# A two-layer hybrid decoder trunk on one core: the mixer's border and first levels in another order, 64 standing columns at the level of 64, and four long products ahead of the four short ones where weights stand

## The reference

```
x = x + 0.5 * rmsnorm(swiglu(rmsnorm(x, g1), w_gate, w_up, w_down), p1)          # 1024 -> 2816 -> 1024
z = rmsnorm(x, g2) @ w_in            # retention q,k,v,gate | GLA q,k,v, low-rank gate, gate
ro = retention(rope(rq), rope(rk) * 64**-0.5, rv)       # 4 heads, keys 64, values 128, fixed decay
log_a = log_sigmoid(ga @ w_a2 + b_a2) / 16
go = gla(gq * 64**-0.5, gk, gv, log_a)                  # 4 heads, decay that depends on the data
x = x + rmsnorm(concat([rmsnorm(ro) * silu(rg), rmsnorm(go) * silu(gg)]) @ w_out, p2)
x = x + rmsnorm(cross_attention(rmsnorm(x, g3), rmsnorm(mem, gm), w_q, w_kv, w_o), p3)   # 4 heads
x = x + 0.5 * rmsnorm(swiglu(rmsnorm(x, g4), ...), p4)
```

## Time and profile before

| | us |
|---|---|
| median of 3 runs | 1184.18 (1184.04 to 1184.34) |
| the profiled execution | 1184.15 |
| its span in the trace | 1182.1 |
| TensorE busy | 1172.7 (99%) |
| VectorE busy | 841.4 (71%) |
| ScalarE busy | 702.6 (59%) |
| GpSimd busy | 150.4 (13%) |
| long products, weights standing in feed-forward, L760 | 864 |
| short ones, L761 | 864 |
| the same in column passes, L639 and L643 | 256 and 256 |

### The profile page before, as it was taken

One profiled execution on the slowest core, in us unless ns is written; L12 is line 12 of the kernel. 1 busy time (PEld: TensorE's weight loads), 2 busy tenths in 40 slices (PEclk: granted clock), 3 DMA queues, 4 the chain that ended last, 5 costly groups with the idle time before them and its releaser, 6 DMA issues. The chain is left out here.

```text
span 1182.1 us, 17336 instructions
## 1 busy us (share of the span) xinstructions
PE 1172.7 (99%) x6164; PEld 997.3 (84%) x6164; DVE 841.4 (71%) x1300; ACT 702.6 (59%) x1225; POOL 150.4 (13%) x220
## 2 busy tenths in 40 slices
PE   9999999999999999999999999999999999999998
PEld 7888888788888888888888888887888888888886
DVE  6866656888767678775487875479887676777752
ACT  7655545756666557654476764376567565666641
POOL 3000002573100100000000000036431001000000
PEclk9999999999999999999999999999999999999999
DMA  9756554454545365555465555554545454555540
GB/s 358 271 184 235 194 202 160 175 179 143 195 144 178 131 204 199 178 201 209 142 214 193 198 196 196 196 201 138 179 154 185 144 177 146 202 187 183 201 168 35
DMA packets 33411, 217.92 MB, mean 184 GB/s; under 512 B 3952, under 2 KB 4208, under 8 KB 9792
## 3 DMA queue, kind: packets, MB, share of 16 engines
q1 hardware_dynamic: 33200, 216.90, 53.7%
q10 hardware_dynamic: 144, 0.13, 0.0%
HBM read 215.97 MB, written 1.05 MB: 184 GB/s over the span
## 5 line engine op out<-in xcount | busy, mean ns | idle before, releaser
L1539 DVE SCALAR_TENSOR_TENSOR w_lo<-raw,first,w_hi 128x512 fp32r<-128x512 f32 x576 | 417.2, 779 | 81.4 <-ACT w_hi L1089 80.2
L1089 ACT ACTIVATE w_hi<-raw,first 128x512 fp32r<-128x512 f32 x568 | 369.1, 716 | 90.3 <-PE acc L761 47.0
L760 PE MATMUL acc<-xT,w_hi 128*128 128x512 f32 x864 | 300.2, 391 | 0.0
L761 PE MATMUL acc<-xT,w_lo 128*128 128x256 f32 x864 | 241.9, 280 | 0.0
L585 PE MATMUL acc<-w_hi,xT 128*128 128x512 f32 x576 | 227.4, 395 | 0.0
L589 PE MATMUL acc<-w_lo,xT 128*128 128x512 f32 x576 | 224.6, 390 | 0.7 <-DVE w_lo L1539 0.7
L586 PE MATMUL acc<-w_hi,xT 128*128 128x512 f32 x576 | 224.4, 390 | 0.0
L760 PEld LDWEIGHTS acc<-xT,w_hi 128*128 128x128 f32 x864 | 161.6, 187 | 35.4
L1531 DVE TENSOR_TENSOR w_lo<-raw,w_hi 128x1024 fp32r<-128x1024 f32 x112 | 124.6, 1146 | 87.5 <-ACT w_hi L1083 87.2
L761 PEld LDWEIGHTS acc<-xT,w_lo 128*128 128x128 f32 x864 | 163.3, 189 | 0.1
L1083 ACT ACTIVATE w_hi<-raw 128x1024 fp32r<-128x1024 f32 x112 | 106.6, 991 | 92.2 <-PE acc L589 75.5
(11 more groups left out here) (219 smaller groups left out, 1377.8 us busy)
## 6 DMA issues: line engine op xcount, KB each, us to landing
raw<-in_gu SPq DMA_DIRECT2D x86, 1024.0 KB, 5.1
raw<-in_down SPq DMA_DIRECT2D x32, 1024.0 KB, 4.8
raw<-in_in SPq DMA_DIRECT2D x24, 1024.0 KB, 5.1
raw<-in_kv SPq DMA_DIRECT2D x16, 1024.0 KB, 5.2
raw<-in_down SPq DMA_DIRECT2D x16, 768.0 KB, 4.2
raw<-in_out SPq DMA_DIRECT2D x8, 1024.0 KB, 5.1
raw<-in_q SPq DMA_DIRECT2D x8, 1024.0 KB, 5.1
raw<-in_o SPq DMA_DIRECT2D x8, 1024.0 KB, 5.1
```

Source lines behind the costliest of these rows:

```text
L760: pe.matmul(o[:, :], w_hi[:, slot, kk, c:c + P], xT[:, :, k, :], start=k == 0, stop=False)
L761: mm = pe.matmul(o[:, TOK:2 * TOK], w_lo[:, slot, kk, c:c + P], xT_hi[:, k, :], start=False, stop=k == KD - 1)
L1089: act.activation(w_hi[:, slot, k, :], raw[:, slot, k, :], ACT.Copy, scale=gains[:, ds(g, 1)]).then_inc(s_hi, 1)
L1539: dve.scalar_tensor_tensor(w_lo[:, slot, k, :], raw[:, slot, k, :], gains[:, ds(g, 1)], w_hi[:, slot, k, :].bitcast(F32), ALU.mult, ALU.su ...
```

## The change

1. TensorE: `x_transposes(l, 1, 1)` goes in ahead of k = 6 instead of k = 5 of the mixer's second pass. VectorE: `w_lo` parts 0 and 1 of the second half of `C_IN + 1` come ahead of `x_norm(l, 1, 1)`, parts 2 and 3 behind it.
2. Retention's second scores and the level of 128 (`second_keys`) go from the middle of pass 5 to its end, the level of 64 from the end of pass 5 to the middle of pass 6. VectorE: the first two `w_lo` parts of the second half of `C_IN + 3` come ahead of `retention_mask(1)` and `level_out(0)`, the others behind them.
3. At the level of 64 only the first 64 positions stand, the result has 64 rows, and VectorE takes it over with a plain copy of 64 rows instead of the masked copy of 128.
4. Where weights stand, each half of a chunk (four k) is four long products and then four short ones, in every pass.

```diff
@@ column_pass
                             pe.matmul(o[:, :], w_hi[:, slot, k, c:c + P], src[:, :, 4 * h + k, :],
                                       start=h == 0 and k == 0, stop=False)
+                        for k in range(4):
                             if t == 0 and mt == 0:
-                                pe.wait_ge(s_lo, low)
+                                pe.wait_ge(s_lo, 4 * half_no(l, ci, h) + k + 1)
                             mm = pe.matmul(o[:, TOK:2 * TOK], w_lo[:, slot, k, c:c + P], src[:, 0, 4 * h + k, :],
@@ feature_chunk
                             pe.matmul(o[:, :], w_hi[:, slot, kk, c:c + P], xT[:, :, k, :], start=k == 0, stop=False)
-                            mm = pe.matmul(o[:, TOK:2 * TOK], w_lo[:, slot, kk, c:c + P], xT_hi[:, k, :],
-                                           start=False, stop=k == KD - 1)
+                            if kk < 3:
+                                continue
+                            for k_lo in range(k - 3, k + 1):
+                                mm = pe.matmul(o[:, TOK:2 * TOK], w_lo[:, slot, k_lo % 4, c:c + P], xT_hi[:, k_lo, :],
+                                               start=False, stop=k_lo == KD - 1)
@@ level
-                            mm = pe.matmul(mb[e][:, c:c + 64], tile, later, start=True, stop=True)
+                            keys = 64 if b == 64 else P
+                            mm = pe.matmul(mb[e][0:keys, c:c + 64], tile[:, 0:keys], later, start=True, stop=True)
@@ mixer, TensorE
-                    if ks == 5:
+                    if ks == 6:
                         x_transposes(l, 1, 1)
-                inside = {4: {4: gqk_transposes}, 5: {4: second_keys}, 7: {4: lambda: levels(l, 2)},
+                inside = {4: {4: gqk_transposes}, 6: {4: lambda: level(l, 1, True, True)}, 7: {4: lambda: levels(l, 2)},
-                behind = {4: lambda: retention_scores(0), 5: lambda: level(l, 1, True, True), 10: gated_outputs,
+                behind = {4: lambda: retention_scores(0), 5: second_keys, 10: gated_outputs,
@@ level_out, VectorE
+                        if b == 64:
+                            dve.tensor_copy(dst[0:64, :, 0, :], src[0:64, :, 0, :]).then_inc(s_mf[e], 1)
+                            continue
@@ mixer, VectorE
+                split_lo(l, C_IN + 1, 1, ks=(0, 1))
                 x_norm(l, 1, 1)
-                split_lo(l, C_IN + 1, 1)
+                split_lo(l, C_IN + 1, 1, ks=(2, 3))
...
+                split_lo(l, C_IN + 3, 1, ks=(0, 1))
                 retention_mask(1)
                 level_out(0)
-                split_after(4)
+                split_lo(l, C_IN + 3, 1, ks=(2, 3))
```

## The result

The changed kernel takes 1194.64 us (median of 6 runs, from 1193.77; one of them took 2386.52 us, about twice as long, and is left out of the ratio; the median of the other five is 1194.57), the kernel before 1184.26 us in the same comparison (1184.04 to 1184.71). The ratio is 1.0086, 95% interval 1.0072 to 1.0100: **slower by 10.4 us**, where 1185.1 (1179.8 to 1188.2) was forecast. The profiled execution took 1194.97 us, its span is 1192.9 us.

What follows compares the result with a forecast made beforehand. TensorE, busy 99% of the span at full clock, was taken as the bound. From 1184.15 us, -2.45 (mixer) +3.9 (feed-forward order) -0.5 (column passes) gave 1185.1 us, range 1179.8 to 1188.2.

Steps and rivals of the forecast that it cites:

- The copy that replaces the masked one is off TensorE's path.: At the level of 64, VectorE's new copy was taken not to delay TensorE; no time was priced for it.
- 0.15 us to spare: At the second level of a later group, GpSimd's operands were reckoned ready at 252.32, TensorE's start about 252.47.
- Part 4: Four long, four short: eight products take 1.405 us; +3.9 us in feed-forward, -0.5 us in column passes.
- Both rivals on part 4: Eight products take 1.387 us everywhere (1180.0 us, chance 0.33), or feed-forward falls to 1.413 us (1187.3 us, chance 0.18).
- The border: In the mixer's second pass, TensorE's stall behind VectorE's norm goes: 0.6 us gained in layer 0, 0.45 in layer 1.
- Scores and the level of 128: Twelve token products later, GpSimd's operands are ready at the level of 128: 0.7 us of waiting gone per layer.
- It just fits: At the level of 64, VectorE empties both banks by 235.9 us, just before TensorE comes at about 236.2.
- 64 standing columns: At the level of 64, halving standing columns saves 0 to 0.45 us; 0.25 us a layer was taken.
- The cap by GpSimd: In the levels, GpSimd's chain lets TensorE gain at most 0.78 us a layer of 0.95 offered; 0.7 taken, border outside.
- the mixer's 2.45 us: Total gain forecast in the mixer: 0.6 + 0.45 at the border plus 2 x 0.7 from scores and levels.
- The third rival: GpSimd's chain does not follow; TensorE gains 0.15 us on it a layer, mixer 1.35 us, time 1186.2; chance 0.10.
- The forecast is wrong if … GpSimd's wait at a level exceeds 0.5 us: A sign of failure at the mixer's levels; a new wait of up to 0.3 us was expected at the third group.

Runs made afterwards that it cites:

- h1: The changed kernel with the old masked copy of 128 rows put back at the level of 64; 1185.91 us (1.0021).
- e3: The kernel before with only the four-long, four-short order of products added; 1186.94 us (1.0023).
- f4: The changed kernel with the old masked copy of 128 rows and the old alternation of long and short products; 1182.94 us (0.9991).
- h5: The kernel before with four long, four short, but eight and eight in the two middle passes of each feed-forward chunk; 1186.02 us (1.0015).
- e1: The changed kernel with long and short products alternating again as before; 1192.29 us (1.0063).
- e2: The changed kernel with a masked 64-row copy in place of the plain one at the level of 64; 1195.59 us (1.0093).
- e4: The kernel before with only the 64 standing columns and the plain 64-row copy at the level of 64; 1190.96 us (1.0060).
- f1: The kernel before with only the plain 64-row copy at the level of 64; 1190.27 us (1.0045).
- f3: The changed kernel with a one-element copy over 128 rows behind the second 64-row copy; 1195.84 us (1.0101).
- g1: The kernel before with the plain 64-row copy at the level of 64 for the second bank only; 1192.18 us (1.0059).
- g2: The kernel before with the plain 64-row copy at the level of 64 for the first bank only; 1191.11 us (1.0062).
- g4: The kernel before with the masked copy at the level of 64 cut to 96 rows; 1190.69 us (1.0061).
- h4: The changed kernel with four one-element 128-row copies in the middle of the eight w_lo operations; 1194.01 us (1.0084).
- f2: The kernel before with only the 64 standing columns at the level of 64, old masked copy kept; 1183.78 us (0.9997).
- g3: The kernel before with a plain copy of all 128 rows at the level of 64; 1183.82 us (0.9999).
- h2: f4 with four long, four short products in the column passes alone; 1182.12 us (0.9986).
- h3: The kernel before with each masked copy at the level of 64 made as two, rows 0 to 63 and 64 to 127; 1184.59 us (1.0004).
- h6: The kernel before with a one-element 64-row copy added behind the copies of the level of 64; 1184.62 us (1.0004).

## Why the prediction was wrong

**The step that failed** is one sentence of part 3: "The copy that replaces the masked one is off TensorE's path." It was priced at nothing, without naming what VectorE and GpSimd do behind it. The copy itself is off the path. But as it goes over fewer rows, VectorE's eight `w_lo` behind it run without giving GpSimd a turn, and one multiply of GpSimd takes 6.07 us instead of 1.2. GpSimd's chain has 0.15 us to spare one group later, a slack that the prediction itself worked out; a delay of 4.9 us is on TensorE's path at once, and TensorE's slower clock behind its waits adds to it. Cost: 8.7 us (the changed kernel against h1). The trace of before could not show it, since the kernel before has no such copy at this place. What it did show was that at this place both engines ran at 1.0 to 1.2 us an operation, which reads as taking turns, and that GpSimd needs these turns. A bound on what the edit costs if it loses them, eight `w_lo` at 0.66 us, could have been written down.

The Trainium skill, SBUF — State Buffer, section "Who interferes with whom", says that VectorE and GpSimd share a pair of ports as an exclusive lock, held for a whole instruction, for which a VectorE operation with two SBUF inputs contends. The kernel before agrees that the two slow each other (1.0 to 1.2 us each where an undisturbed one takes 0.66 to 0.74). It does not show that they exclude each other for the whole of a record: from 238.60 to 246.55 eight `w_lo` and six operations of GpSimd fit into 7.95 us, which one after the other, at 0.67 and 0.7 us, would take 9.6. By the same section of the Trainium skill the one that issues first gets the pair, and the other waits for that instruction. That would bound the loss to one `w_lo`, 0.7 us. The trace differs: the multiply stands at 236.99, the first of the `w_lo` at 237.11, and the multiply is held up over all eight. The measurement decides.

Point by point:
- *Part 4:* right. Eight products take 1.4034 us, forecast 1.405. 216 x 16.4 ns = 3.5 us, columns 64 x -0.010 = -0.6: 2.9 us where the sum had 3.4; measured 2.7 (e3) and 1185.91 - 1182.94 = 3.0 (h1 and f4, from two sets). h5 shows the reason given, that a run pays for the change of width, by halving the changes.
- *Both rivals on part 4* fell with that: 1.387 and 1.413 us do not occur in the changed kernel. The section "Back-to-back issue gap" of the Trainium skill's page TensorE: Matmul & The Clock Gate, by which the order would be free, is not borne out: 0.23% for part 4 alone.
- *The border:* the mechanism right. The wait for `w_lo` is gone in both layers, and the transposes don't wait for the norm. They start at 202.23, with no gap. The size was put too low: TensorE's lead in f4 grows by 0.80 us in layer 0 (0.13 of it ahead of the border) and by 0.78 in layer 1 up to the start of the stretch named above, where the sum had 0.6 and 0.45.
- *Scores and the level of 128:* right on the wait, which is gone. "It just fits" held too: no wait of TensorE for `pg` at the level of 64 in the changed kernel.
- *64 standing columns:* the mechanism right, the size at the edge: 0.43 us a layer of 0 to 0.45, where I took 0.25. The Trainium skill's section "LDWEIGHTS" of the same page, by which the load goes with the standing columns, gave about 0.4 and was nearer.
- *The cap by GpSimd:* wrong, and this is what a kernel without the starvation would have shown. The sum had 0.7 us a layer from scores and levels; f4's trace gives 0.10. Against that the border gave more than its share, so that the mixer's 2.45 us became 1.2 by the medians. The prediction lets GpSimd's multiply move forward by 0.63 us; its rows give 245.87 - 245.34 = 0.53 up to the end of TensorE's group. In f4 the multiply does start right behind its exponents (245.07). But those end at 245.11, only 0.23 us earlier than before, though the first exponents had started 0.66 us earlier (225.73 against 226.39): on the way more of GpSimd's operations run beside `w_lo`, the second exponent for 1.08 us instead of 0.63. So the border's gain is not outside this cap, as was assumed. TensorE then waits 0.22 and 0.64 us in each layer. The third rival (the mixer gives 1.35, since GpSimd eats the rest), with a chance of 0.10, describes it. With h1's 1185.91 the forecast would have been off by 0.8 us, and that would have been partly luck: 1.2 us too much gain from the levels would have stood against 0.4 to 0.5 too little from the border and 0.4 too much cost of part 4.
- *"The forecast is wrong if … GpSimd's wait at a level exceeds 0.5 us"*: it is 1.74 us, and also stands at two levels.

In sum: 1185.1 + 8.7 for the starved GpSimd, + 1.25 for the mixer's smaller gain (2.45 - 1.2), - 0.4 for part 4 (3.4 less 3.0) = 1194.6 us. The terms are differences of the same runs, so the sum closes by itself; what is shown independently is each term's place in the traces.

**What stays open** is why fewer rows do this. Starved: every kernel whose level of 64 is copied out of PSUM with its upper rows (64 or 96 to 127) left out, in one bank or in both, plain or masked, in the old order of the work and in the new (after, e1, e2, e4, f1, f3, g1, g2, g4, h4). Not starved: every kernel that goes over all the rows there (before, e3, f2, f4, g3, h1, h2, h3, h5, h6). That is shown, in both layers of each one's trace (one profiled execution of each kernel). The moment at which the two engines meet does not part the two lists: GpSimd's operation starts 0.09 us behind the first `w_lo` in f1 and e4 (starved), 0.09 and 0.10 behind it in before and g3 (not), 0.12 ahead of it in the changed kernel (starved) and 0.21 ahead in h1 (not). Whether the state is set by the long 64-row read of PSUM, and why a 128-row operation behind it doesn't clear it (g2, f3) while a break in the stream does (h4), was not settled.

## What to carry to other kernels

Where GpSimd and VectorE share work, don't price an edit on VectorE by its own duration: ask whether GpSimd still gets its turns in the stream of two-input operations behind it, and what TensorE waits for if it gets none. An operation over half the rows took as long as one over all of them here, so cutting rows on VectorE alone has nothing to give and this to lose. A wait of TensorE of 1.5 to 2 us can cost far more than its length, as the clock behind it may fall: the same 1.96 us cost 1.8 in one layer of e4 and 4.9 in the other. And long and short products are best left in the pairing that settles: four and four cost 16 ns more for eight products than the settled pairs of the feed-forward blocks (1403 against 1387), and 10 ns less than the pairs of the column passes (1413).

## What the runs showed of the hardware

- VectorE's two-input stream kept one GpSimd operation (0.61 to 0.74 us alone) waiting over eight instructions, 5.75 to 6.16 us in nine kernels, behind a copy that left rows 64 to 127 or 96 to 127 out, and never behind one that went over all rows.
- Four one-element operations in the stream, 0.32 us, ended that, and the engines shared the time from there (0.9 to 1.2 us an operation).
- A plain copy of 64 rows out of PSUM took as long as one of 128 (0.74 us for two).
- Loads of 64 standing columns let 64-column products follow each other in 52 + 7 ns a pair of records, instead of 105 + 7.
- Runs of long products behind short ones start 233, 236, 228 and 233 ns apart and settle at 226 to 227 only from the sixth on (h5).
- After a wait of TensorE of 1.96 us the granted clock stayed at 1.00 in layer 0 and fell to the lower level in layer 1 of the same execution (e4); after 1.74 and 1.44 us in a row it was 0.50 for a stretch of 5 us (changed kernel).
